# Expert slots laid out per token tile: one sorted region for each half of the sequence, gather tile by tile, scatter in four row tiles of 32

## What is computed

```
g_idx = argmax(t @ w_group + b_group)             # one of 4 groups
top_v, top_i = top_k(logits of that group, 2)     # 2 of its 4 experts
gates = softmax(top_v) * softmax(group)[g_idx]
out = sum over the 16 experts of (silu(t @ Wg[e]) * (t @ Wu[e]) * gate[:, e]) @ Wd[e]
```

## Time and profile before

| | us |
|---|---|
| median of three runs (lowest to highest) | 730.14 (729.5 to 730.46) |
| the profiled execution | 729.28 |
| its span, first to last instruction | 727.5 |
| PE busy | 707.7 (97%) |
| DVE, ACT, POOL busy | 277.8, 149.2, 26.4 |
| moved by DMA | 250.89 MB, mean 345 GB/s |

### The profile page before, as it was taken

The page is one execution under the profiler, slowest core; times in us unless marked ns, Lnnn a source line. Parts: engine busy times, 40 slices in busy tenths (PEclk is TensorE's granted clock), DMA queues, the critical chain, the costliest instruction groups (busy, mean ns, idle before and its releaser), DMA issues.

```text
span 727.5 us, 8400 instructions
## 1 busy us (share of the span) xinstructions
PE 707.7 (97%) x3182; PEld 329.6 (45%) x3182; DVE 277.8 (38%) x683; ACT 149.2 (21%) x365; POOL 26.4 (4%) x47
## 2 busy tenths in 40 slices
PE   9999999999999999989999999999999999998996
PEld 6488454564333333333445545464333333332344
DVE  1213361544427242422322557363435424242224
ACT  3000241341111111110331144242111111110132
POOL 0600000000000000000000000000000000000000
PEclk9999999999999999999999999999999999999999
DMA  9997448869999999999999851569999999999941
GB/s 344 373 294 283 183 173 326 341 241 410 425 420 421 419 423 419 421 420 423 401 381 408 341 204 71 185 242 387 421 422 420 421 420 422 421 420 422 405 163 59
DMA packets 50666, 250.89 MB, mean 345 GB/s; under 512 B 4713, under 2 KB 5961, under 8 KB 26049
## 3 DMA queue, kind: packets, MB, share of 16 engines
q1 hardware_dynamic: 48256, 245.04, 84.1%
q0 software_dynamic: 2048, 5.07, 2.3%
q10 hardware_dynamic: 320, 0.22, 0.1%
HBM read 247.15 MB, written 4.73 MB: 346 GB/s over the span
## 4 chain that ended last, share of the span: by engine, by line
PE 85%; DMA 7%; issue 2%; SPq 2%; DVE 2%; ACT 1%; POOLq 0%; POOL 0%; ACTq 0%; DVEq 0%
PE bank L981 26%; PE bank L666 24%; PE bank L998 13%; DMA weights<-in_moe_w_down_dram 7%; PE bank L699 4%; PE bank L1019 4%; PE bank L941 2%; PE bank L893 2%; SPq L438 2%; PE bank L651 2%; PE bank L990 1%; PE bank L679 1%; PE bank L805 1%; PE bank L737 0%; PE bank L1241 0%
## 5 line engine op out<-in xcount | busy, mean ns | idle before, releaser
L981 PE MATMUL bank<-weights,expert_rows 128*64 128x512 f32 x1024 | 227.0, 593 | 6.8 <-DMA weights<-in_moe_w_up_dram 6.8
L666 PE MATMUL bank<-weights,normalised 128*128 128x512 f32 (+1 forms) x448 | 191.4, 580 | 0.9 <-DVE normalised L1637 0.7
L981 PEld LDWEIGHTS bank<-weights,expert_rows 128*64 128x64 f32 x1024 | 74.5, 137 | 149.9 <-issue 149.7
L666 PEld LDWEIGHTS bank<-weights,normalised 128*128 128x128 f32 x448 | 83.1, 190 | 91.4 <-issue 88.5
L998 PE MATMUL bank<-weights,hidden_turned_odd 128*64 128x512 f32 x256 | 58.8, 598 | 0.7 <-DMA weights<-in_moe_w_down_dram 0.7
L998 PE MATMUL bank<-weights,hidden_turned 128*64 128x512 f32 x224 | 51.5, 598 | 1.3 <-DVE hidden_turned L1957 0.6
L1477 ACT ACTIVATE gate_tanh<-bank 128x256 f32<-128x256 f32 x32 | 12.3, 384 | 190.5 <-PE bank L981 190.5
L1339 ACT ACTIVATE expert_outputs<-bank 128x512 fp32r<-128x512 f32 x32 | 19.1, 597 | 123.4 <-PE bank L998 123.4
L1987 DVE TENSOR_TENSOR gather_onehots<-bank,expert_outputs 128x512 fp32r<-128x512 f32 x32 | 22.1, 692 | 55.6 <-ACT expert_outputs L1339 55.5
L1957 DVE COPY hidden_turned<-bank 128x256 f32<-128x256 f32 x16 | 6.8, 424 | 78.5 <-PE bank L990 78.5
L1957 DVE COPY hidden_turned_odd<-bank 128x256 f32<-128x256 f32 x16 | 6.8, 425 | 78.2 <-PE bank L990 78.2
(11 more groups left out here) (265 smaller groups left out, 591.1 us busy)
## 6 DMA issues: line engine op xcount, KB each, us to landing
weights<-in_moe_w_gate_dram SPq DMA_DIRECT2D x64, 1024.0 KB, 16.0
weights<-in_moe_w_up_dram SPq DMA_DIRECT2D x64, 1024.0 KB, 16.9
weights<-in_moe_w_down_dram SPq DMA_DIRECT2D x60, 1024.0 KB, 19.8
weights<-in_even_w_in_dram SPq DMA_DIRECT2D x5, 2048.0 KB, 21.0
weights<-in_ple_w_gate_dram SPq DMA_DIRECT2D x4, 2048.0 KB, 31.3
weights<-in_even_w_out_dram SPq DMA_DIRECT2D x2, 2048.0 KB, 31.3
weights<-in_odd_w_qkv_dram SPq DMA_DIRECT2D x2, 2048.0 KB, 19.6
weights<-in_odd_w_out_dram SPq DMA_DIRECT2D x2, 2048.0 KB, 19.7
```

What stands on the lines that cost most here:

```text
L666: mm = pe.matmul(B[bank][:, 0:width], XT[:, k, tok(t)], w[:, k, :], start=(k == 0), stop=(k == KD - 1))
L981: mm = pe.matmul(bank[j * BLK:(j + 1) * BLK, :].rearrange("p (m f) -> p m f", m=2), rows[:, k, :], W[:, slots, a:a + FF // 2], start=(k == ...
```

## The change

Slots are counted within a token tile: two regions of 256 slots, each sorted by expert. A block of an expert is 32 rows of tile 0 and 32 rows of tile 1 (`ROWS = 32`); extra blocks would be needed from 33 rows of an expert in one tile. Slots, one-hots, gather and table of tile 0 no longer depend on tile 1.

```diff
-def rows_bank(k):
-    return (0, 1, 2, 3, 4, 5, 4, 7)[k]
+def rows_bank(t, j):
+    return ((2, 3, 4, 5), (0, 1, 2, 3))[t][j]
+def tile_rows(t, half):
+    a = BLK * half + ROWS * t
+    return slice(a, a + ROWS)
...
@@ sync queue, experts: after the side stores and the load of XD
                         sp.wait_ge(sem("seeded"), 4 * l + 2)
-                        outside(2)
+                        outside(3)
                         for half in range(2):
                             load_part(3, 1, half)
                             load_part(4, 0, half)
                             if half == 0:
                                 sp.wait_ge(sem("seeded"), 4 * l + 4)
-                                outside(3)
+                                outside(2)
+                        for half in range(2):
                             load_part(4, 1, half)
                             load_part(3, 2, half)
...
@@ tensor queue, experts
+                def slot_sums(t):
+                    low, one = C[:, C_LOW:C_LOW + P], C[:, C_ONE:C_ONE + P]
+                    a = 2 * NE * t
+                    pe.wait_ge(sem("chosen"), 4 * l + 2 * t + 1)
+                    pe.matmul(B[1][:, a:a + NE], low, chosen(t), start=True, stop=False)
+                    pe.wait_ge(sem("chosen"), 4 * l + 2 * t + 2)
+                    pe.matmul(B[1][:, a:a + NE], one, SUMS[t], start=False, stop=True)
+                    pe.matmul(B[1][:, a + NE:a + 2 * NE], one, SUMS[t], start=True, stop=True).then_inc(sem("slots_ready"), 1)
+                def gathered(t, j):
...
+                    for k in (2 * j, 2 * j + 1):
+                        for part in range(2):
+                            mm = pe.matmul(B[rows_bank(t, j)][:, (k - 2 * j) * SEQ:(k - 2 * j + 1) * SEQ], HSP[part][:, t, k:D:KD],
+                                           PH[:, t, :], start=(part == 0), stop=(part == 1))
...
-                def scatter(par, t, stop=False, ready=None):
+                def scatter(par, part, t, stop=False):
+                    for half in range(2):
+                        r = tile_rows(t, half)
+                        mm = pe.matmul(B[sum_bank(t, half)][:, :], PT2[r, par, :], (YS, PHT)[part][r, par, :], start=False, stop=stop)
+                    return mm
...
-                gathered_first(0)
-                gathered_first(1)
-                for k in range(4, 6):
-                    gathered(k)
...
-                open_sums(0)
-                first_rows(0)
-                open_sums(1)
-                for k in range(6, KD):
-                    gathered(k)
-                first_rows(1)
+                side_part(0, 0, 0)
+                transposes(kn, 1, (6, 7))
+                slot_sums(0)
+                side_part(0, 0, 1)
+                logits(1, 0)
+                logits(1, 1)
+                side_part(0, 1, 0)
+                whole_logits(1)
+                side_part(0, 1, 1)
+                gathered(0, 0)
+                gathered(0, 1)
+                side_part(1, 0, 0)
+                slot_sums(1)
+                side_part(1, 0, 1)
+                gathered(0, 2)
+                gathered(0, 3)
+                side_part(1, 1, 0).then_inc(sem("first_weights_used"), 1)
+                gathered(1, 0)
+                gathered(1, 1)
+                side_part(1, 1, 1)
+                gathered(1, 2)
+                gathered(1, 3)
...
+                open_sums(1)
+                first_rows(0)
...
+                open_sums(0)
                 other_rows(0)
                 spread()
+                first_rows(1)
                 other_rows(1)
...
@@ scalar queue, experts
+                act.wait_ge(sem("first_weights_used"), l + 1)
+                for e in range(2):
+                    tile_copy(e, 0, offs[e][0], first)
+                side_evac(1, 0)
+                act.wait_ge(sem("table_ready"), 3 * l + 2)
+                for e in range(2):
+                    offs[e].append(offset(e, 1))
+                rows_evac(1, 0)
+                act.wait_ge(sem("rows_by_act"), 4 * l + 3)
+                act.wait_ge(sem("rows_by_dve"), 4 * l + 1)
+                for e in range(2):
+                    tile_copy(e, 1, offs[e][1], first).then_inc(sem("xe_first"), 1)
+                side_evac(1, 1)
                 act.wait_ge(sem("side_first_stored"), 16 * (l + 1))
...
+                rows_evac(1, 2)
...
+                seed(1)
...
+                seed(0)
...
@@ vector queue, experts
+                rows_evac(1, 1)
+                rows_evac(0, 2)
+                rows_evac(0, 3)
                 dve.wait_ge(sem("side_first_stored"), 16 * (l + 1))
-                rows_evac(1)
-                rows_evac(3)
+                rows_evac(1, 3)
```

More of the change, by code:

```diff
@@ L915, in experts @@
                 pe.wait_ge(sem("side_weights_landed"), 32 * (l + 1))
-                side_part(0, 0, 0)
-                transposes(kn, 1, (6, 7))
-                side_part(0, 0, 1)
-                logits(1, 0)
-                logits(1, 1)
-                side_part(0, 1, 0)
-                whole_logits(1)
-                low, one = C[:, C_LOW:C_LOW + P], C[:, C_ONE:C_ONE + P]
-                pe.wait_ge(sem("chosen"), 3 * l + 1)
-                pe.matmul(B[1][:, 0:3 * NE], one, SUMS0, start=True, stop=False)
@@ L926, in experts @@
-                pe.matmul(B[1][:, 0:NE], low, chosen(0), start=False, stop=False)
-                side_part(0, 1, 1)
-                side_part(1, 0, 0)
-                pe.wait_ge(sem("chosen"), 3 * l + 2)
-                pe.matmul(B[1][:, NE:2 * NE], low, chosen(1), start=False, stop=False)
-                pe.wait_ge(sem("chosen"), 3 * l + 3)
-                pe.matmul(B[1][:, 0:3 * NE].rearrange("p (n e) -> p n e", n=3), one,
-                          SUMS1.unsqueeze(1).to_broadcast([P, 3, NE]), start=False, stop=True).then_inc(sem("ranks_ready"), 1)
@@ L970, in spread @@
-                    for c in range(4):
-                        mm = pe.matmul(B[7][:, tok(c)], RT[:, 86 + c:87 + c].to_broadcast([P, P]), ident, start=True, stop=True)
+                        for q in range(4):
+                            a = (474, 476, 86, 88)[c] + q % TT
+                            mm = pe.matmul(B[4][ROWS * q:ROWS * (q + 1), tok(c)], RT[:, a:a + 1].to_broadcast([P, ROWS]), ident,
+                                           start=True, stop=True)
                     mm.then_inc(sem("srow_ready"), 1)
@@ new lines, in offset, with tile_copy, rows @@
+                def offset(e, t):
+                    return act.value_load(TBL[0:1, NE * t + e:NE * t + e + 1], min_val=0, max_val=LAST)
+                def tile_copy(e, t, off, part=slice(0, KD)):
+                    return copy(XE[:, e % 2, part, ROWS * t:ROWS * (t + 1)], XS[t][:, part, bass.ds(off, ROWS)])
+                def rows(e):
+                    offs = [offset(e, t) for t in range(TT)]
+                    act.wait_ge(sem("gate_up_ready"), NE * l + e - 1)
+                    for t in range(TT):
+                        i = tile_copy(e, t, offs[t])
+                    i.then_inc(sem("xe_ready"), 1)
@@ new lines, in experts @@
+                act.wait_ge(sem("logit_parts"), 2 * l + 2)
+                side_evac(0, 0)
+                side_evac(0, 1)
+                rows_evac(0, 0)
+                rows_evac(0, 1)
+                first, rest = slice(0, KD // 2), slice(KD // 2, KD)
+                act.wait_ge(sem("table_ready"), 3 * l + 1)
+                offs = [[offset(e, 0)] for e in range(2)]
+                act.wait_ge(sem("rows_by_act"), 4 * l + 2)
+                act.wait_ge(sem("first_weights_used"), l + 1)
@@ L1467, in experts @@
+                act.wait_ge(sem("rows_by_dve"), 4 * l + 4)
+                for e in range(2):
+                    for t in range(TT):
+                        i = tile_copy(e, t, offs[e][t], rest)
+                    i.then_inc(sem("xe_ready"), 1)
+                seed(0)
                 act.wait_ge(sem("srow_ready"), l + 1)
-                copy(SROW.rearrange("p c s -> p (c s)"), B[4][:, :])
-                act.activation(WROW.rearrange("p c s -> p (c s)"), B[7][:, :], ACT.Copy, scale=0.5).then_inc(sem("srow_copied"), 1)
+                copy(SROW.rearrange("p c s -> p (c s)"), B[4][:, 0:SEQ])
@@ L1471, in step @@
+                act.activation(WROW.rearrange("p c s -> p (c s)"), B[4][:, SEQ:2 * SEQ], ACT.Copy, scale=0.5).then_inc(sem("srow_copied"), 1)
                 def step(e):
@@ new lines, in onehot_rows, with table @@
+                def onehot_rows(t):
+                    dve.wait_ge(sem("iota_ready"), 2 * l + 1)
+                    then(dve.tensor_scalar(TMP[t], IOTA, SL[:, 1, t:t + 1], None, ALU.is_equal))
+                    dve.scalar_tensor_tensor(out=PH[:, t, :], in0=IOTA, scalar=SL[:, 0, t:t + 1], in1=TMP[t],
+                                             op0=ALU.is_equal, op1=ALU.add).then_inc(sem("onehots_ready"), 1)
+                def table(t):
```

(10 more changed lines are left out.)

283 lines of the change are left out of this document (136 added, 147 removed).

## The result

The changed kernel takes 736.19 us (median of four runs, 736.03 to 736.73) against 730.01 us of the kernel before, run beside it: ratio 1.0092, with a 95% interval from 1.0079 to 1.0105. The forecast was 737.9 us with a range from 732.5 to 741. The profiled execution took 736.14 us, its span 734.3.

A forecast was written before the change was run, and what follows sets the result against it. Full DMA transfers were taken to bound each layer's experts, so their later start costs +3.9 us a layer, twice +7.8: profiled 729.28 becomes 737.1, median 737.9 us. Range 732.5 to 741.

The forecast's parts named there:

- T: End of `first_rows(0)`, which frees the first half slots for loading; forecast at 158.6 us in layer 0, 1.5 later.
- X: Issue of the load of `XD` in SP's queue; forecast at 157.3 us in layer 0, 6.2 later.
- The gather's price: A PE gather matmul of 256 columns costs 0.23 us, bounds 0.21 to 0.245, against 0.245 for 512 columns.
- The shift of 3.9 us: Later landing in each layer: 157.3 + 3.7 us for 1.57 MB of transfers - 157.1; twice, +7.8 us.
- Without a hole from X: Claim that transfers run full from the load of `XD` on, with 1.57 MB more before them.
- sum of bytes: Layer's expert weights: 80.2 MB left at 157.1 us, 191 us at 420 GB/s, giving an end at 350 us.
- the three upward terms: Upper bounds per layer: gather price +0.4, slot sums and DVE +0.8, ACT's chain +0.5 us.
- the cover: Shorter scatter on PE counts nothing for the end while transfers set it; PE just waits longer for weights.
- Rival A: Gather's weight load hides behind the stream, 256 columns cost about half of 0.245 us; 733.3 us; chance 0.11.
- B: Rival: PE sets the experts' end, so its shorter work saves about 8.5 us a layer; 713 us; chance 0.06.
- C: Rival: holes in the engines behind the first freed half slot absorb the later start; 730 us; chance 0.05.
- D: Rival: an expert needs an extra block in a layer, some 20 us each; 757 us; chance 0.02.

The follow-up runs named there:

- the side-by-side run: Changed kernel with high and low rows kept in the order of k, so a gather's 128 stationary columns are neighbours; 734.64 us, ratio 1.0078.
- the last experiment: Changed layout, strided weight loads, only three gather groups ahead of first_rows(0), load to `H` behind four first halves, no side-store wait; 733.03 us, ratio 1.0047.
- after, early: Changed kernel with the last two side products right behind the sixth, ahead of later gathers, and ACT's copies moved forward; 735.51 us, ratio 1.0088.
- order: Changed kernel, strided loads: side products ahead of last 24 gathers, two gather groups behind first_rows(0), copies and seeds earlier, no side-store wait; 737.57 us, ratio 1.012.
- the load to `H` late: The reordered changed kernel with strided loads, and the load to `H` moved behind two second halves of expert weights in SP's queue; 737.32 us, ratio 1.0107.

## Why the prediction was right, and where it was off

The reading that carried it was that each layer's experts end with the last down weights, that the transfers are full from T on, and that the change moves X more than T. Step by step:

- The gather's price, 0.23 us: measured 0.225, for the reason given (the load at a step of eight, 337 ns).
- The last side product at 152.7: 153.03. The end of ACT's copy at 154.0: 154.09. X at 157.3: 157.35. T at 158.6: 158.87. The first part to `H` at 158.3: 158.13.
- The shift of 3.9 us in layer 0: 3.66. "Without a hole from X" was not quite so, as there are 301 GB/s from 158 to 162 us; but before had 338 there. That the two nearly cancel is luck, as the prediction worked out neither. Its sum of bytes gave 350 us for a landing at 351.94 and was called closed; the 1.9 us left over are half of the forecast shift, and it is the windows and the late side product, not that sum, that bear out the reading.
- The shift of 3.9 us in layer 1 is the term that was mis-sized: 3.01. It isn't the times of X and T: less the start and the 3.66 us of layer 0 they moved by 6.06 and 1.57 us, in layer 0 by 6.04 and 1.54. The same count of bytes over 32 us gives 49 GB/s or 3.7 us. The remaining 0.7 us is no higher rate later: from 120 us behind layer 0's landing to the landing in layer 1, before moved 85.97 MB (401 GB/s) and after 85.64 (394 GB/s). The kernel before had thus moved 0.33 MB more, 0.8 us at 420 GB/s, when its last down weights were in. I take this for part of the loads behind them; what held back the last piece isn't shown. Without the wait for the store it landed 0.5 us earlier in the kernel before, at the same T.
- The bounds: the three upward terms (0.4, 0.8, 0.5) make 1.7 us, so the layer's upper bound is 5.6 us, not 5.3, and the upper end 741.3. It decides nothing, as the time lies below the forecast.
- The scatter: eight matmuls 0.66 us instead of 1.14, and an expert 11.56 us of PE instead of 12.0. All of it ended as waits for weights, from 6.8 to 26.0 us at line 979, as the cover said.
- Rival A: refuted by 0.225 us, and the side-by-side run shows what its premise would have needed. B: refuted by 27 us of PE added for nothing. C: refuted by the landing. D: no extra block.

"Nothing later brings it back" held. What the prediction didn't see is that the 3.7 us behind X have a wait of their own inside, and that T's successor is a third moment: where X and T were moved forward, these, a slower rate of transfer and, in six of the profiles, some 1.7 us of a lower granted clock ate the gain. The theory is good for what a late X costs; it promises too much for an early one. No version of the changed layout beat the kernel before; the nearest are 0.2% slower, which is about what the clock cost in their profiles. Open are the low rate in the last experiment, what makes the clock fall in one execution and not in another, and the part of layer 1's shift that no window holds.

## What to carry to other kernels

In a stretch where transfers are full, count the bytes that are left when it begins: whatever delays the first loads beyond the time that they have to spare is paid in full, and whatever shortens the engines' work inside it is paid back as waits. So when independent work is used to fill an engine's gaps, look at what waits for that work's result; here one 0.86 us product stood ahead of a store, its completion and 1 MB of weights. And before moving a load forward, follow the queue to the next two waits behind it. When a variant misses, compare the length of the same matmuls and the granted clock between the two traces first: a fall of the clock can be mistaken for what the edit did.

## What the runs showed of the hardware

- A weight load of 128 float32 columns takes 337 ns at a step of eight elements and 188 side by side. The same step costs ACT 2.18 us for 1.16 in a copy of 1024 columns.
- Four row tiles of 32 do the scatter's eight matmuls of 512 columns in 0.66 us, two of 64 in 1.14.
- A load of 1.05 MB issued to idle engines lands 4.7 to 4.9 us later, 2.5 of them its bytes at 420 GB/s. The Trainium skill, "DMA: Bandwidth & Descriptors", section "Anatomy of one DMA — SWDGE (gpsimd) path", puts about 2 us on a transfer issued by GpSimd, most of it for the confirmation of the last byte. For these loads, which SP issues, the trace agrees in size and not in place: behind X of the kernel after, 16 GB/s flow in the first microsecond, 156 in the second and 401 in the third. In "after, early" the last data moved before 157.8 us and the landing is at 158.07, so most of the 2 us lies ahead of the data. The same load issued beside an unfinished store of 0.5 MB took 6.2 us (last kernel; the row of its issue, KB, us to landing, with that of after above it):

```profile
weights_rest<-in_moe_w_down_dram SPq DMA_DIRECT2D x1, 1024.0 KB, 4.8
```

```profile
weights_rest<-in_moe_w_down_dram SPq DMA_DIRECT2D x1, 1024.0 KB, 6.2
```

- In the profile of "order" the granted clock is 0.71 in the four microseconds from 162 us on, behind PE's two waits of 0.87 and 0.94 us, so part of them ran at 1.2 instead of 2.4 GHz, and 16 matmuls that take 3.65 us at full clock took 5.35. With the load to `H` late the same two waits (0.88 and 0.95 us) were followed by full clock in layer 0. Eight matmuls between the layers took 5.40 instead of 3.70 us, and four ahead of the router 3.66 instead of 1.96: about 1.7 us each time.
- The four times of "order" go with the mean granted clock of their executions: 733.92 us at 0.997, 736.02 at 0.994, 739.72 at 0.991 and 739.13 at 0.989. In "after, early" it is 733.45 at 0.998, 734.88 at 0.996, 736.14 at 0.993 and 738.03 at 0.991. The kernel before kept 0.997 to 0.999 in all its executions. So the wide spread of such variants, and with it part of their medians, goes with the clock; that the clock is the whole of it isn't shown.
